# Five of eight row blocks of fifteen modulation chunks weighted and summed on POOL

## The reference

```
def first_block(...):
    silu_c = jax.nn.silu(c)
    for i in range(DEPTH):                       # 2 layers
        mod = silu_c @ ada_w[i] + ada_b[i]       # [1,1024] @ [1024, 6*1024]
        sh1, sc1, g1, sh2, sc2, g2 = split(mod, 6)
        h = rms_norm(x, norm_mix_g[i]) * (1.0 + sc1) + sh1
        x = x + g1 * attention(h, ...)
        h = rms_norm(x, norm_ffn_g[i]) * (1.0 + sc2) + sh2
        x = x + g2 * grouped_moe(h, ...)
# second_block: the same with w_mod, for the vectors c and c_ctx, then the hybrid layer
```

## Time and profile before

| what | value |
|---|---|
| median of 3 runs | 1597.2 us (1596.63 to 1603.7) |
| the profiled execution | 1605.66 us, span 1603.9 us |
| PE busy | 1514.8 us, 94% |
| DVE busy | 599.2 us, 37% |
| ACT busy | 417.7 us, 26% |
| POOL busy | 62.6 us, 4%, 79 instructions |
| DMA moved | 535.35 MB, mean 334 GB/s |

### The profile page before, as it was taken

One profiled execution on the slowest core, in us unless ns is written; L12 is line 12 of the kernel. 1 busy time (PEld: TensorE's weight loads), 2 busy tenths in 40 slices (PEclk: granted clock), 3 DMA queues, 4 the chain that ended last, 5 costly groups with the idle time before them and its releaser, 6 DMA issues.

```text
span 1603.9 us, 24144 instructions
## 1 busy us (share of the span) xinstructions
PE 1514.8 (94%) x9543; PEld 836.0 (52%) x9543; DVE 599.2 (37%) x1383; ACT 417.7 (26%) x956; POOL 62.6 (4%) x79
## 2 busy tenths in 40 slices
PE   7999999999999999999998999889999999999997
PEld 3665664444446647544443866557554444434433
DVE  3453552322354263533323165433433322332232
ACT  1142331212132433412111433353212121121121
POOL 0000010000010001100000044001000000000000
PEclk9999989999999999999999999799999999999999
DMA  9998779999999778799999300612799999999995
GB/s 353 351 337 299 299 294 423 422 422 422 422 384 342 281 296 320 314 422 422 422 422 408 120 1 1 255 60 93 288 421 422 422 422 422 422 422 423 422 422 241
DMA packets 122474, 535.35 MB, mean 334 GB/s; under 512 B 11023, under 2 KB 14953, under 8 KB 73266
## 3 DMA queue, kind: packets, MB, share of 16 engines
q1 hardware_dynamic: 122002, 534.40, 83.1%
q10 hardware_dynamic: 416, 0.17, 0.0%
HBM read 533.48 MB, written 1.06 MB: 333 GB/s over the span
## 4 chain that ended last, share of the span: by engine, by line
PE 66%; DMA 26%; DVE 3%; ACT 2%; issue 1%; SPq 1%; POOL 0%; DVEq 0%; POOLq 0%; ACTq 0%
PE pair L1047 17%; DMA ring<-in_w_dram 16%; DMA ring<-in_moe_w_gate_dram 8%; PE bank L769 7%; PE pair L1071 4%; PE bank L1071 3%; PE pair L1149 3%; PE bank L666 3%; PE bank L1033 2%; PE bank L863 2%; PE bank L1085 2%; PE bank L776 2%; PE pair L745 2%; DMA ring<-in_a_w_qkv_dram 1%; PE bank L1149 1%; PE bank L1024 1%
## 5 line engine op out<-in xcount | busy, mean ns | idle before, releaser
L1047 PE MATMUL pair<-ring,arena 128*64 128x512 f32 x2048 | 455.5, 595 | 30.4 <-DMA ring<-in_w_dram 21.6
L1047 PEld LDWEIGHTS pair<-ring,arena 128*64 128x64 f32 x2048 | 140.8, 137 | 313.3 <-issue 271.1
L2432 DVE SCALAR_TENSOR_TENSOR xT<-bank,mod,xT 128x256 f32<-128x256 f32 x180 | 75.9, 477 | 171.5 <-PE bank L1085 171.5
L1071 PE MATMUL pair<-ring,arena 128*64 128x512 f32 x512 | 127.1, 619 | 2.1 <-ACT arena L1772 2.1
L1071 PE MATMUL bank<-ring,arena 128*64 128x512 f32 x512 | 121.1, 593 | 0.0
L769 PE MATMUL bank<-hh,ring 128*128 128x256 f32 x512 | 117.3, 386 | 2.0 <-DMA ring<-in_a_w_qkv_dram 2.0
L769 PEld LDWEIGHTS bank<-hh,ring 128*128 128x128 f32 x512 | 96.8, 192 | 24.2 <-issue 8.6
L2418 DVE SCALAR_TENSOR_TENSOR arena<-sq,arena,pair 128x512 f32<-128x512 f32 x32 | 35.6, 1113 | 175.6 <-PE pair L1047 175.6
L1772 ACT ACTIVATE arena<-pair 128x512 f32<-128x512 f32 x32 | 19.1, 597 | 266.7 <-PE pair L1109 266.7
L2426 DVE TENSOR_TENSOR arena<-pair,arena 128x512 f32<-128x512 f32 x32 | 22.1, 692 | 159.9 <-ACT arena L1778 159.9
L1033 PE MATMUL bank<-arena,hh 128*128 128x128 bf16 x928 | 81.0, 219 | 0.2 <-DVE arena L2296 0.2
(11 more groups left out here) (419 smaller groups left out, 1891.3 us busy)
## 6 DMA issues: line engine op xcount, KB each, us to landing
ring<-in_w_dram SPq DMA_DIRECT2D x192, 1024.0 KB, 23.1
ring<-in_moe_w_gate_dram SPq DMA_DIRECT2D x64, 1024.0 KB, 17.4
ring<-in_moe_w_up_dram SPq DMA_DIRECT2D x64, 1024.0 KB, 17.9
ring<-in_moe_w_down_dram SPq DMA_DIRECT2D x64, 1024.0 KB, 18.4
ring<-in_ada_w_dram SPq DMA_DIRECT2D x24, 2048.0 KB, 17.2
ring<-in_w_mod_dram SPq DMA_DIRECT2D x12, 2048.0 KB, 12.3
ring<-in_a_w_qkv_dram SPq DMA_DIRECT2D x6, 2048.0 KB, 20.3
ring<-in_b_w_qkv_dram SPq DMA_DIRECT2D x6, 2048.0 KB, 19.9
```

The lines of the kernel that those rows point to most:

```text
L1047: last = mm(b[2 + m][half(a), :], x_sel[:, k, half(a)], R8[moe_slot(l, a, m)][:, k, :], start=(k == 0), stop=(k == KT - 1))
L1071: last = mm(b[5 + n][half(a), :], hidT[:, f, half(a)], R4[moe_slot(l, a, 2)][:, f, n * 512:(n + 1) * 512], start=(f == 0), stop=(f == FT - 1))
L2432: last = stt(xT[:, k, :], (sums_last if last_pair else sums)[r][:, k % 2 * S:(k % 2 + 1) * S], mod[:, l, G2 + k:G2 + k + 1], xT[:, k, :], ...
```

## The change

Fifteen chunks that PE did alone, with eight matmuls, are now treated much like the twelve of DVE, by POOL: 8, 10, 12, 14 to 19 in layer 0 and 28, 31 to 35 in layer 1. Once the chunk has landed, POOL multiplies blocks 3 to 7 by their elements of the vector (five `tensor_scalar` of 128x512, each in place), then adds blocks 4 to 7 to block 3 (four `tensor_tensor` of 128x512, each waiting for the one before it). PE does blocks 0 to 2 as before, waits for `pool_rows`, and closes the chunk with one matmul of the sum against ones. POOL takes the chunks in order: the nine of layer 0 ahead of its first two `sum_squares`, the six of layer 1 ahead of the next two. The semaphore `top_ready` is given up, and its two counts a layer are put on `h_tok_ready`; the waits on it are renumbered.

```
+        POOL_FIRST = 3
         PRODUCTS = {4: 3, 5: 3, 6: 3, 7: 3, 11: 3, 13: 3, 20: 3, 21: 3, 22: 3, 23: 3, 29: 3, 30: 3}
+        POOLED = (8, 10, 12, 14, 15, 16, 17, 18, 19, 28, 31, 32, 33, 34, 35)
+        pooled_at = lambda g: (2 * (KT - POOL_FIRST) - 1) * (POOLED.index(g) + 1)
 
         def mod_products(g):
-            n = PRODUCTS.get(g, KT)
+            n = POOL_FIRST if g in POOLED else PRODUCTS.get(g, KT)
             parts = [(k, k % 4) for k in range(n)]
             return parts if n == KT else parts + [(n, g % 4 if n == 0 else 3)]
...
                 for k, q in mod_products(g):
                     row = c_[:, k, 31 - r:63 - r]
-                    if k == PRODUCTS.get(g, KT):
+                    if g in POOLED and k == POOL_FIRST:
+                        pe.wait_ge(table_in, 16)
+                        pe.wait_ge(pool_rows, pooled_at(g))
+                        row = K(C_WIN + 31 - r, 32)
+                    elif k == PRODUCTS.get(g, KT):
...
-                pe.wait_ge(h_tok_ready, turn(h_tok_ready, 4))
+                pe.wait_ge(h_tok_ready, 6 * l + 4)
...
-                    fn(tok_part(0, t), by_block(h_tok[:, t, :]), ACT.Copy).then_inc(top_ready, 1)
+                    fn(tok_part(0, t), by_block(h_tok[:, t, :]), ACT.Copy).then_inc(h_tok_ready, 1)
...
+            def weighted_rows(g):
+                n = mod_at[g]
+                pool.wait_ge(full[slot_of_chunk(n)], 16 * (n // NSLOT + 1))
+                w, (c_, _) = R8[slot_of_chunk(n)], mod_window(g)
+                total = w[:, POOL_FIRST, :]
+                for k in range(POOL_FIRST, KT):
+                    nc.gpsimd.tensor_scalar(w[:, k, :], w[:, k, :], c_[:, k, 31:32], None, ALU.mult).then_inc(pool_rows, 1)
+                for k in range(POOL_FIRST + 1, KT):
+                    pool.wait_ge(pool_rows, pooled_at(g) - KT + k)
+                    nc.gpsimd.tensor_tensor(total, total, w[:, k, :], ALU.add).then_inc(pool_rows, 1)
+
+            pool.wait_ge(csil_ready, 1)
+            for g in POOLED:
+                if g < 20:
+                    weighted_rows(g)
             sum_squares(KT, 0)
             sum_squares(2 * KT, 7)
+            for g in POOLED:
+                if g >= 20:
+                    weighted_rows(g)
             sum_squares(3 * KT, 14)
             sum_squares(4 * KT, 21)
```

More of the change, by code:

```diff
@@ L301, in program @@
         out_tok = sem("out_tok")
-        top_ready, parts_ready = sem("top_ready"), sem("parts_ready")
+        parts_ready, pool_rows = sem("parts_ready"), sem("pool_rows")
         MOE = []
@@ L1741, in route @@
                     fn(route_gap_exp, route_gap, ACT.Exp).then_inc(gap_exp, 1)
-                act.wait_ge(h_tok_ready, 4 * l + 4)
+                act.wait_ge(h_tok_ready, 6 * l + 4)
                 for t in range(TT):
-                    fn(tok_part(0, t), by_block(h_tok[:, t, :]), ACT.Copy).then_inc(top_ready, 1)
+                    fn(tok_part(0, t), by_block(h_tok[:, t, :]), ACT.Copy).then_inc(h_tok_ready, 1)
             def experts(l):
@@ L2403, in experts @@
                     rest = by_block(h_tok[:, t, :])
-                    dve.wait_ge(top_ready, TT * l + t + 1)
+                    dve.wait_ge(h_tok_ready, 6 * l + 4 + t + 1)
                     then(tt(rest, rest, tok_part(0, t), ALU.subtract))
```

## The result

The changed kernel takes 1683.58 us (median of 4 runs, 1679.68 to 1685.47), the one before 1597.33 us (4 runs, 1596.63 to 1603.7): 1.0528 times as long, interval 1.0503 to 1.0553. I had forecast 1637 us and a range to 1655. The direction was right; the 40 us that I forecast are less than half of the 86 that came. The two profiled executions, 1605.66 and 1684.43 us, stand 78.8 us apart. The medians stand 86 apart, because that of before was profiled 8 us above its median.

What follows compares the result with a forecast made beforehand. PE's row was taken to bound the attention layers, DMA the expert stage. Layer 0 +18.3, layer 1 +18.1 and clock +3.6 gave +40.0 us on the median 1597.2, so 1637 us, range 1612 to 1655.

Steps and rivals of the forecast that it cites:

- Bound and pass-through: Attention layers: PE's row is the bound; gain or loss before out_first(7) moves the expert loads one to one.
- What PE gets back: All fifteen chunks: about 0.86 us of PE time each if the sum is there in time, 12.9 us at most.
- each of them gives its 0.86: Chunks 10, 12, 14, 15, 28, 31 land long before PE wants them, so each saves 0.86 us.
- The place of the loss: PE waits for POOL at chunks 8, 16 to 19 and 32 to 35; the tails cost +18.3 and +18.1 us.
- Multiplies: no row shows a one-input instruction on POOL: POOL's multiply of a block: 0.73 us taken from a 256-column two-input add, between 0.48 and 1.30.
- C: POOL's time for a chunk's nine instructions: 9.5 us forecast, with ends 6.8 and 12.3.
- the sum: Whole kernel: 18.3 for layer 0, 18.1 for layer 1 and 3.6 for the clock, +40.0 us.
- Rival 1: DVE and POOL hold each other up, stretching POOL's instructions some 15%: 1651 us; 0.18 with other ways to longer chunk times.
- two terms of 1.8 for the clock: Behind chunks 19 and 35 the granted clock falls to half on the path: 2 x 1.8 = 3.6 us.
- that expert stages absorb the delay: Rival: waits for POOL come, but slack in the expert stage hides them, about 1597 us; chance 0.05.
- that POOL keeps up: Rival: at the closes of 19 and 35 nothing is lost and PE gains, 1584 us; chance 0.04.
- Cheap multiplies: Rival: POOL's multiply is near its floor, a chunk takes 6.8 to 8.5 us, 1614 to 1628 us; chance 0.13.

Runs made afterwards that it cites:

- dve_two: Kernel before, nothing on POOL, with chunks 12 and 28 also summed by DVE in its idle time; 1598.0 us, ratio 1.0004.
- early_only: Changed kernel with only chunks 10, 12, 14, 28 and 31 on POOL, the rest back on PE; 1604.3 us, ratio 1.0036.
- tail_only: Changed kernel with only chunks 16 to 19 and 32 to 35 on POOL, the other seven back on PE; 1675.7 us, ratio 1.0477.
- the run of forms: Kernel before plus three POOL instructions of each form beside chunks 8 to 18, into scratch, for durations only; 1606.9 us in its one run.
- shadow_short: Kernel before, with POOL also doing its nine instructions per chunk into scratch, unawaited by PE, skipping chunks 18, 19, 34, 35; 1612.3 us, ratio 1.0077.
- two_op: Changed kernel with each POOL multiply written as a tensor_scalar of two operations (multiply, plus a zero column); 1644.4 us, ratio 1.0291.

## Why the prediction was wrong

**Bound and pass-through: right.** Expert stages kept their 422 GB/s and their length. The delay of layer 0 was 44.5 us at its second output projection and 44.4 at layer 1's first projection.

**What PE gets back: right as matmul time, wrong as time.** Chunks 10, 12, 14, 15, 28 and 31 run as four matmuls without a wait for POOL. But "each of them gives its 0.86" took PE's row as the only bound. Behind chunk 12 the time saved turns into a wait for DVE (0.81 us in dve_two, 0.56 in the changed kernel), and DVE is slower beside POOL. With five such chunks alone, early_only is 0.36% slower than before, not 4.3 us faster.

**The place of the loss: right.** PE waits at the nine chunks named, and at no other, and takes the last four at POOL's pace. The waits are longer than forecast: 11.6 and 8.1 us at chunks 16 and 32 (8 forecast), 4.1 to 6.2 at the others of the tail (4 to 5), 7.9 at chunk 8 (4). tail_only carries 77 of the 86 us.

**The step that failed is "Multiplies: no row shows a one-input instruction on POOL", 0.73 us, with 1.30 as its upper end.** It measured 1.55. I treated the cost as one that grows with the elements read, so that the two-input add bounded the one-input multiply from above. That argument was no row, and the run of forms refutes it: one operation 1.49 to 1.57, two operations 0.90, two inputs 1.04, all on 512 columns. The adds came at 1.34, start to start, instead of 1.45 (a wait on the instruction ahead costs 0.07 here, not 0.15). Together C is 13.2 and not 9.5. It enters nine times, 9 x 3.7 = 33 of the 39 us by which the profiled executions missed the sum.

The other 6 us, by the earlier trace rows and the timeline above:
- Chunk 8 put projection chunk 1 at 102.95, +8.6 us and not +1.6. C makes 3.7 of the difference. The close at 1.2 GHz takes 1.9 and not 0.9, and the spread and chunk 9 behind it 1.2 and 3.2 us instead of 0.7 and 1.9. I had priced the half clock only behind the last chunks. The projection itself then ran at full clock, 3.72 and not 5.38, which gives 1.7 back.
- PE waited 1.8 us for DVE's stretched step at 113.83. Rival 1 named DVE and POOL holding each other up, but priced it on POOL. POOL's five multiplies took 7.73 to 8.58 us and its four adds 5.28 to 6.38, at most about a fifth more; DVE's steps grew by up to 108%. In a kernel where PE doesn't wait for POOL the same work of POOL costs 7.4 and 3.9 us (shadow_short). That it is hidden behind the waits in the tail of the changed kernel is argued, not shown.
- The closes of 19 and 35 took 1.0 longer each. My two terms of 1.8 for the clock behind them measured about 0.7 and 0.9.
- Chunk 16 took 9.3 us to land instead of 7.8.

These are between profiled executions. The 7 us by which the medians stand further apart are no term of the prediction; what is known of them stands with the result.

**Rivals.** That expert stages absorb the delay, and that POOL keeps up, are both out. *Cheap multiplies* is out for this form: it took 1.55 against DVE's 0.48, while two-input forms took 1.04 and 1.29. The Trainium skill ("GPSIMD Engine Reference", section 4.1, Engine selection) has one-input work on POOL at roughly line rate; this trace disagrees for the one-operation form by a factor of three.

**The range.** It ended at 1655, under the 1662 that the sum gave at its upper end of C, and that end rested on the bound of 1.30. With the measured C of 13.2 the same sum gives 1637 + 33 = 1670, still 14 us under the 1683.6: the 6 us above, and the 7 by which the medians stand further apart than the profiled executions. For the form of two_op, whose multiply is what I had assumed, 1644 us lies inside the range.

## What to carry to other kernels

Work moved to a slower engine has two tests: does each piece end before its use, and is its time below the spacing at which pieces arrive when they come in a row. Here the spacing was 5 us and the piece took 13. An instruction form that no row shows has no upper bound from another form; three of them run beside the kernel in a scratch area give it in one run. Before POOL gets work, look at what DVE does at that time: steps with two SBUF inputs took 56% to 108% longer here, those with an input from PSUM didn't. And time taken off an engine counts only if the next thing in its row is ready earlier too; else it turns into a wait, as behind chunk 12.

## What the runs showed of the hardware

- POOL, 512 columns of float32: tensor_scalar with one operation 1.49 to 1.59 us, with two operations 0.76 (128 partitions, back to back) to 0.90, tensor_tensor multiply 1.04, add 1.29, copy 0.61, memset 0.53. One operation with 256 columns 0.93, with 128 0.71. (Adds on 128 partitions; copy, memset and the shorter columns on 64; the one-operation form and the multiply of two tensors on both.)
- A spread (stride 0) second input costs POOL nothing: 1039 against 1040 ns.
- On DVE beside a reading POOL, two-SBUF-input steps of 128 columns took 731 ns instead of 351, of 256 columns 745 instead of 478; beside memsets 352 and 480.
- In the changed kernel, after PE's waits of 5 to 12 us for POOL, the granted clock was 0.50 for the next 3 to 6 us, and a lone closing matmul took 1.88 us.
